# Where the weights' low parts and the feed-forward's square are made in a two-block transformer kernel

## What is computed

```python
def second_block(x, p, positions, ...):
    h = x
    for i in range(2):
        u = rms_norm(h, g_mix_pre[i])
        y = stick_breaking_attention(u, ...) if i == 0 else dilated_attention(u, ...)
        h = h + rms_norm(y, g_mix_post[i])
        u = rms_norm(h, g_ffn_pre[i])
        f = jnp.square(jax.nn.relu(u @ w_ff_in[i])) @ w_ff_out[i]     # 1024 -> 4096 -> 1024
        h = h + rms_norm(f, g_ffn_post[i])
        gate = jax.nn.sigmoid(rms_norm(h, g_ple[i]) @ w_ple_gate[i])
        h = h + (p[i] @ w_ple[i]) * gate
    return h
```

## Time and profile before

| | us |
|---|---|
| median of 3 runs | 3079.3 |
| lowest, highest | 3075.21, 3086.74 |
| the profiled execution | 3081.43 |
| its span in the profile | 3079.6 |
| TensorE busy (matmuls) | 2912.4 |
| VectorE busy | 1820.4 |
| ScalarE busy | 1295.7 |
| GpSimd busy | 275.1 |

### The profile page before, as it was taken

The page is one execution under the profiler, slowest core; times in us unless marked ns, Lnnn a source line. Parts: engine busy times, 40 slices in busy tenths (PEclk is TensorE's granted clock), DMA queues, the critical chain, the costliest instruction groups (busy, mean ns, idle before and its releaser), DMA issues.

```text
span 3079.6 us, 43537 instructions
## 1 busy us (share of the span) xinstructions
PE 2912.4 (95%) x17549; PEld 2347.7 (76%) x17549; DVE 1820.4 (59%) x3091; ACT 1295.7 (42%) x2091; POOL 275.1 (9%) x148
## 2 busy tenths in 40 slices
PE   6989999999999899999999989999998998999998
PEld 4966554446677688785888758889997997987997
DVE  5457857654434777635577755689643555545554
ACT  3134321134453533325252156587544444334444
POOL 2000000000000000000000000000030442320442
PEclk8999999999999999999999999999999999989999
DMA  7312324423334222232223432445642664422662
GB/s 260 96 55 83 96 96 137 123 72 123 124 114 168 75 96 96 84 94 83 83 69 102 125 105 91 143 160 162 189 137 83 183 180 129 137 76 79 181 180 91
DMA packets 419626, 366.74 MB, mean 119 GB/s; under 512 B 20261, under 2 KB 392582, under 8 KB 419172
## 3 DMA queue, kind: packets, MB, share of 16 engines
q1 hardware_dynamic: 416928, 359.11, 37.7%
q0 software_dynamic: 1472, 4.47, 0.4%
q10 hardware_dynamic: 1028, 0.39, 0.1%
HBM read 360.80 MB, written 3.15 MB: 118 GB/s over the span
## 4 chain that ended last, share of the span: by engine, by line
PE 78%; DVE 10%; ACT 5%; issue 5%; DMA 1%; POOL 0%; SPq 0%; POOLq 0%; DVEq 0%; ACTq 0%
PE banks L920 7%; PE banks L1065 6%; PE banks L1067 6%; PE banks L1066 5%; PE banks L1193 5%; PE banks L934 4%; PE banks L936 4%; PE banks L935 4%; PE banks L1033 3%; PE banks L1449 3%; PE banks L1458 3%; ACT narrow_hi L1701 1%; PE banks L1324 1%; PE banks L1254 1%; PE banks L1156 1%
## 5 line engine op out<-in xcount | busy, mean ns | idle before, releaser
L2514 DVE TENSOR_TENSOR narrow_lo<-wring,narrow_hi 128x1024 fp32r<-128x1024 f32 (+1 forms) x212 | 268.9, 1270 | 378.0 <-ACT narrow_hi L1701 377.7
L1065 PE MATMUL banks<-operand_narrow,narrow_hi 128*128 128x256 f32 x1312 | 388.9, 296 | 22.9 <-POOL narrow_lo L890 10.6
L1701 ACT ACTIVATE narrow_hi<-wring 128x1024 fp32r<-128x1024 f32 (+2 forms) x312 | 309.0, 998 | 224.2 <-PE banks L1067 141.7
L890 POOL TENSOR_TENSOR narrow_lo<-wring,narrow_hi 128x1024 fp32r<-128x1024 f32 x100 | 251.2, 2514 | 1402.1 <-ACT narrow_hi L1701 1402.1
L1066 PE MATMUL banks<-operand_narrow,narrow_hi 128*128 128x256 f32 x1312 | 372.7, 284 | 0.0
L1067 PE MATMUL banks<-operand_narrow,narrow_lo 128*128 128x256 f32 x1312 | 372.6, 284 | 0.0
L1065 PEld LDWEIGHTS banks<-operand_narrow,narrow_hi 128*128 128x128 f32 x1312 | 252.9, 193 | 36.2 <-POOL narrow_lo L890 14.4
L1066 PEld LDWEIGHTS banks<-operand_narrow,narrow_hi 128*128 128x128 f32 x1312 | 253.1, 193 | 1.9 <-issue 0.2
L1067 PEld LDWEIGHTS banks<-operand_narrow,narrow_lo 128*128 128x128 f32 x1312 | 253.0, 193 | 0.0
L1449 PE MATMUL banks<-operand_a,wring 128*128 128x512 f32 (+1 forms) x512 | 173.4, 492 | 1.5 <-DVE conv_in L2764 1.5
L1065 PE MATMUL banks<-ff_h,narrow_hi 128*128 128x256 f32 x512 | 146.4, 286 | 2.5 <-DVE ff_h L3275 1.6
(11 more groups left out here) (487 smaller groups left out, 7015.0 us busy)
## 6 DMA issues: line engine op xcount, KB each, us to landing
wring<-in_w_in_dram SPq DMA_DIRECT2D x52, 1024.0 KB, 5.4
wring<-in_w_ada_dram SPq DMA_DIRECT2D x48, 1024.0 KB, 5.3
wring<-in_ffn_wup_dram SPq DMA_DIRECT2D x44, 1024.0 KB, 5.1
wring<-in_w_ff_in_dram SPq DMA_DIRECT2D x32, 1024.0 KB, 5.5
wring<-in_w_ff_out_dram SPq DMA_DIRECT2D x32, 1024.0 KB, 5.8
wring<-in_ffn_wdown_dram SPq DMA_DIRECT2D x32, 704.0 KB, 4.6
wring<-in_w_in_dram SPq DMA_DIRECT2D x36, 512.0 KB, 5.1
wring<-in_w_in_dil_dram SPq DMA_DIRECT2D x18, 1024.0 KB, 5.0
```

What stands on the lines that cost most here:

```text
L890: pool.tensor_tensor(NL[:, v % 4, 0:kn, :], w, NH[:, v % 4, 0:kn, :].bitcast(F32), ALU.subtract).then_inc(ev("narrow_lo_pool"), 1)
L1065: pe.matmul(out, wh, a[:, 0:SEQ], start=first, stop=False)
L1701: act.activation(dst, src, f, **kw).then_inc(*inc)
L2514: tt(NL[:, v % 4, 0:kn, :], w, NH[:, v % 4, 0:kn, :].bitcast(F32), ALU.subtract).then_inc(ev("narrow_lo"), 1)
```

## The change

1. No weight unit is made low on GpSimd any more: `low_on_pool` and the GpSimd loop go, and VectorE makes all units low, in the order of its calls of `narrow`.
2. In the feed-forward of the second block, VectorE no longer squares. After the relu ScalarE issues two Square operations from the same tile: one that writes the high part of the hidden tile (rounded to fp32r by its output type), and one in place that writes the full square. VectorE's `low_half` waits for both.

```diff
--- before.py
+++ after.py
@@ -412,15 +412,9 @@
 
         return (GLO[:, m, SEQ:512], GLO[:, m, 0:SEQ]) if l else (AH[:, m, :], GLO[:, m, :])
 
-    def low_on_pool(v):
-
-        first = pl.narrow_first["sqk"]
-        return v >= first + 4 and v % 2 == 1
-
     def low_made(v):
 
-        return (ev("narrow_lo_pool") if low_on_pool(v) else ev("narrow_lo"),
-                sum(low_on_pool(i) == low_on_pool(v) for i in range(v + 1)))
+        return ev("narrow_lo"), v + 1
 
     def cn(name, n0=0, n=None):
         late, c0, w = const_at[name]
@@ -883,12 +877,6 @@
         pool.dma_start(X[:, :, :].rearrange("p k n -> p (k n)"), XD).then_inc(ev("x_back"), 16)
         pool.wait_ge(*done(pl.last("down0")))
         pool.memset(WA[0:32, :], 0.0).then_inc(ev("zeroed"), 1)
-        for v in range(len(pl.narrow)):
-            if low_on_pool(v):
-                _, w, kn = narrow_weights(v)
-                pool.wait_ge(ev("narrow_hi"), v + 1)
-                pool.tensor_tensor(NL[:, v % 4, 0:kn, :], w, NH[:, v % 4, 0:kn, :].bitcast(F32),
-                                   ALU.subtract).then_inc(ev("narrow_lo_pool"), 1)
 
 
     @block.tensor
@@ -2368,10 +2356,11 @@
             for h in range(2):
                 for m in range(16):
                     narrow(pl.narrow_first[f"ffin{l}.{h}"] + m, 4 if m < 2 else 3)
-                    act.wait_ge(ev("ff_full"), FT2 * l + 16 * h + m + 1)
+                    act.wait_ge(*freed(F[f"ffin{l}.{h}"] + m))
                     if m == 0 and h:
                         act.wait_ge(pe_done["gemm"], pl.narrow_done[pl.narrow_first[f"ffout{l}.0"] + 15])
-                    op(HN[:, m, 0:SEQ], TD[:, 2 + m % 2, 0:SEQ], ACT.Copy, (ev("ff_hi"), 1))
+                    op(HN[:, m, 0:SEQ], TD[:, 2 + m % 2, 0:SEQ], ACT.Square, (ev("ff_hi"), 1))
+                    op(TD[:, 2 + m % 2, 0:SEQ], TD[:, 2 + m % 2, 0:SEQ], ACT.Square, (ev("ff_full"), 1))
 
                 def both(m):
                     t = F[f"ffout{l}.{h}"] + m
@@ -2507,8 +2496,6 @@
             while n_narrow[0] <= u + more and narrow_near(n_narrow[0], u):
                 v = n_narrow[0]
                 n_narrow[0] += 1
-                if low_on_pool(v):
-                    continue
                 _, w, kn = narrow_weights(v)
                 dve.wait_ge(ev("narrow_hi"), v + 1)
                 tt(NL[:, v % 4, 0:kn, :], w, NH[:, v % 4, 0:kn, :].bitcast(F32), ALU.subtract).then_inc(ev("narrow_lo"), 1)
@@ -3272,6 +3259,7 @@
 
                 def low_half(m):
                     dve.wait_ge(ev("ff_hi"), FT2 * l + 16 * h + m + 1)
+                    dve.wait_ge(ev("ff_full"), FT2 * l + 16 * h + m + 1)
                     tt(HN[:, m, SEQ:512], TD[:, 2 + m % 2, 0:SEQ], HN[:, m, 0:SEQ].bitcast(F32),
                        ALU.subtract).then_inc(ev("ff_h"), 1)
 
@@ -3287,8 +3275,6 @@
                     if m == 0 and h == 0:
                         scale(F[f"fpre{l}"])
                     stt(x, bank(t, 0, SEQ), 0.0, RS, ALU.max, ALU.mult).then_inc(*free(t))
-                    dve.wait_ge(*freed(t))
-                    tt(x, x, x, ALU.mult).then_inc(ev("ff_full"), 1)
                 low_half(15)
```

## The result

The changed kernel took **3111.91 us** (median of 4 runs, 3108.51 to 3114.86), the kernel before 3079.54 beside it. The ratio is 1.0106, with a 95% interval of 1.0089 to 1.0124: slower by about 1.1%, 2.6 us above the forecast and inside its range.

The account below looks back on a forecast made before the run. Four ffin stages were taken as bound by the round trip between VectorE and ScalarE, the rest mostly by TensorE. 28.4 + 3.2 - 0.4 - 1.2 = +30.0 us on 3079.3 gave 3109.3 us, range 3092 to 3123.

Parts of the forecast that it names:

- The loop: Feed-forward's first product (ffin): VectorE and ScalarE wait for each other in every tile, 3.68 us from relu to relu.
- the ring: The closed chain of waits between VectorE and ScalarE in ffin, 3.68 us from one relu to the next.
- The stage: One ffin stage, first relu to matmul on hidden tile 15: 47.75 to 54.8 us, +7.1, +28.4 for four.
- C: Much slower: TensorE's gaps in every ffin tile let its clock fall, +71 us on top, 3180 us; chance 0.04.
- pg0: Gate stage with the same kind of wait chain, sigmoid in place of the Squares: 17.6 to 20.8 us, +3.2.
- pg1: Gate stage where no units follow: last tiles wait for TensorE, unit 5 comes early, end moves by -0.4 us.
- The start of dqk: TensorE's 2.37 us wait for GpSimd's unit shrinks as idle VectorE makes it in 1.23: -1.2 us.
- What was put at nothing: Stages sqk, sv, dqk, dv and ffout: no such loop closes there, so no change in time.
- A: Faster: ScalarE's high part need not wait behind the Squares, TensorE sets ffin's pace, 3067 us; chance 0.04.
- B: No measurable change: ffin's loop closes but both Squares are covered, 3.35 to 3.45 us a round, 3090 us; chance 0.08.

Follow-up runs that it names:

- the reordered runs: Changed kernel with ScalarE's second Square behind the weight unit's high part: 3098.69 us; changed kernel with VectorE's unit behind the relu in ffin: 3066.08 us.
- the open order: Changed kernel with VectorE's unit in each ffin tile behind the relu instead of ahead of the low part and relu: 3066.08 us, ratio 0.9960.

## Why the prediction was right

**The loop.** Forecast 3.68 us a round, found 3.63 to 3.64. Each step agrees within 0.02: the two Squares stand 0.32 and 0.31 from what follows them, where I had taken 0.33 and 0.32. The estimate that I had set beside it from the Trainium skill's "ScalarE: Activation LUTs" (section "What ACT_TABLE_LOAD costs"), 0.31 us a Square and 2 us less in the sum, is borne out by both numbers. That the ring sets the time, and not an engine, is shown by the reordered runs: 0.31 us out of the ring is 0.31 us out of the round, and with the ring open 46 us are gone with the same work on every engine.

**The stage.** From relu 0 (2374.17) to TensorE's first matmul on hidden tile 15, which is this row of its timeline, it is 54.25 us, forecast 54.8:

```profile
2428.42 0.39 PE L1053 MATMUL banks<-ff_h,narrow_hi 128*128 128x256 f32 x1 [1.00 <-DVE ff_h L3263]
```

That is +6.5 a stage and +26.0 for four, where I had +28.4.

**What the sum left out.** The feed-forwards lost 28.9 us, not 26.0. The missing 2.9 is the clock. Behind two of the four stages TensorE, after its waits for the last hidden tiles (1.58 and 1.00 us in ffin0.1), ran at a granted clock of 0.90 and then 0.68 for four microseconds each, shown above for ffin0.1; its matmuls are 0.21 us apart there. From the first matmul on hidden tile 15 to the next row scale or relu these two took 46.0 and 46.9 us, against 44.5 and 45.4 in the kernel before: 1.5 each, 3.0 in sum. The waits of ffin0.0 are as long (1.66 and 1.00) and have no dip behind them. In the kernel before no window of 4 us at those four places is below 1.00. I had the clock as an all-or-nothing rival (C, +71); what it does here is a small toll at the end of a stage. Two errors of the stage term, -2.4 and +2.9, cancelled; that the sum came so close is luck.

**pg0** was put at +3.2. The first and the last scaled tile of VectorE's timeline, answering to the earlier trace rows, are 21.08 us apart, so +3.5:

```profile
2603.16 0.42 DVE L3311 TENSOR_TENSOR tmp_act<-banks,gate_rank 128x256 f32<-128x256 f32 x1
...
2624.24 0.42 DVE L3311 TENSOR_TENSOR tmp_act<-banks,gate_rank 128x256 f32<-128x256 f32 x1
```

The round is 3.37 where I added up 3.31. **pg1** was put at -0.4 and came to +0.3 (13.78 to 14.12), a miss of 0.7 in a small term. **The start of dqk** was put at -1.2. From the last scaled tile of pg0 to TensorE's first matmul with a unit there it went from 23.14 us to 21.78, so -1.4, and the agreement is luck. The kernel before, profiled again, has 22.28: 0.9 of it is a difference between two executions of one kernel. Before its wait for the unit TensorE waits for ScalarE's `b_qk`, 3.27 us before and 3.26 after; for the unit itself it waited 0.46 us, and the step from there to the unit's matmul went from 1.13 us to 0.63. So a faster unit gave 0.5, and the term was over twice too large: the sum left out that another wait ends just ahead of this one. The matmuls behind it are still 0.21 us apart, as I had left it.

**What was put at nothing** stayed within scatter: the stretch with dqk and dv is 0.6 us shorter, the unit's 0.5 among them, and the one with sqk and sv 0.3 longer. Between sv's end and the first feed-forward 1.6 us came in, but the kernel before, profiled again, has the same 1.5: not the change.

**The rivals.** A had TensorE set the pace by itself, as follows if the engine that is twice as fast simply takes over. Both engines' loads would have allowed it, and the open order shows it; the old order forbade it. B needed the ring to hide the Squares. It didn't: all six steps are there in line. C happened in small, as said. The forecast's reason, the closed ring of 3.68, was the case. Its total of +30.0 stands against +32.4 by the medians. The profiled execution has +27.1, which is +35.1 in the second block less the 8.0 of the first; in that block 26.0 + 2.9 + 3.5 - 1.4 + 0.3 = 31.3 are accounted for by name (0.9 of the -1.4 not being the change's), and the other 4 lie between the stages: the 1.6 ahead of the first feed-forward, and 2.3 behind the second beyond pg1's 0.3, where the clock falls in some executions and not in others.

## What to carry to other kernels

When two engines pass tiles to each other in program order, add up the ring before you weigh the loads: an operation that is moved to a faster engine can land inside the ring, and then it costs its full length in every round, however idle the engine. The cure is to issue the operation that somebody waits for first, and the one with slack (here a weight unit needed three tiles later) behind it; that line alone was worth 46 us here, and in the old order the move of the units lost, with the square on either engine. Look at who waits for whom on both timelines in one round; the name of the engine that TensorE waits for (GpSimd before, VectorE after) pointed at neither cause.

## What the runs showed of the hardware

- VectorE's operations with two inputs in SBUF and GpSimd's exclude each other in whole operations: 0.42 us became 2.12 and 2.32 behind a GpSimd operation of 2.4 to 2.9 us, and a unit of 1.23 us became 1.91 in the kernel before. Relus with one input in PSUM kept 0.41. I had the 1.91 in my sum, as a number without its cause. The other way round GpSimd's unit took 3.48 us behind VectorE's of 1.22.
- After waits of 1.0 to 1.7 us at a stage's end TensorE's matmuls ran 0.21 us apart for a while in some stages, at a cost of 1.5 us each, and not in others that look alike (two of four in the changed kernel).
- An execution can have its first block, which is the same in all these kernels, up to 11 us longer or shorter than another (2219.0 to 2230.4 us); two executions of one kernel differed by 1.7 and 2.7.
